# Positions instead of weights stand still in four feed-forward stages, and their product is turned on TensorE

## What is computed

```python
def swiglu(h, w13, w2):
    gate, up = jnp.split(h @ w13, 2, axis=-1)      # w13: 1024 x 5632, w2: 2816 x 1024
    return (jax.nn.silu(gate) * up) @ w2

def second_block(x, mem, positions, ...):
    for l in range(2):
        h = rms_norm_2(x, ffn1_norms[l, 0])
        x = x + 0.5 * rms_norm_2(swiglu(h, ffn1_w13[l], ffn1_w2[l]), ffn1_norms[l, 1])
        ...                                        # token mixing, cross attention
        h = rms_norm_2(x, ffn2_norms[l, 0])
        x = x + 0.5 * rms_norm_2(swiglu(h, ffn2_w13[l], ffn2_w2[l]), ffn2_norms[l, 1])
```

## Time and profile before

| | |
|---|---|
| median of 3 runs | 2096.44 us (2095.05 to 2098.67) |
| the profiled execution | 2096.13 us |
| its span, first to last instruction | 2093.9 us |
| TensorE matmul, weight load busy | 97%, 90% |
| VectorE, ScalarE, GpSimd busy | 65%, 52%, 2% |
| share of TensorE in the chain that ended last | 79% |
| weights and inputs moved | 359.30 MB, mean 172 GB/s |

### The profile page before, as it was taken

The page is one execution under the profiler, slowest core; times in us unless marked ns, Lnnn a source line. Parts: engine busy times, 40 slices in busy tenths (PEclk is TensorE's granted clock), DMA queues, the critical chain, the costliest instruction groups (busy, mean ns, idle before and its releaser), DMA issues.

```text
span 2093.9 us, 37767 instructions
## 1 busy us (share of the span) xinstructions
PE 2029.4 (97%) x15428; PEld 1894.5 (90%) x15428; DVE 1363.5 (65%) x1871; ACT 1093.0 (52%) x1702; POOL 52.3 (2%) x50
## 2 busy tenths in 40 slices
PE   7999999999999999999999999999999899998998
PEld 7989988999899889889888998999899898888997
DVE  6786866776566566767767554655477677756554
ACT  5846555554554454456456444644455455545443
POOL 0021000000000000010100000000000011000000
PEclk9999999999999999999999999999999999999999
DMA  7522454555465556434554655555555435444553
GB/s 263 171 74 82 163 186 145 203 188 187 161 221 189 186 179 203 166 111 141 181 201 145 206 184 191 199 183 183 191 183 180 157 111 169 168 166 153 182 189 121
DMA packets 98441, 359.30 MB, mean 172 GB/s; under 512 B 11160, under 2 KB 11480, under 8 KB 98008
## 3 DMA queue, kind: packets, MB, share of 16 engines
q1 hardware_dynamic: 98272, 356.90, 49.9%
HBM read 353.65 MB, written 1.05 MB: 169 GB/s over the span
## 4 chain that ended last, share of the span: by engine, by line
PE 79%; DVE 12%; ACT 6%; issue 2%; DMA 1%; ACTq 0%; SPq 0%; DVEq 0%
PE ps L923 15%; PE ps L924 14%; PE ps L925 14%; PE ps L988 6%; PE ps L989 6%; PE ps L990 6%; PE ps L911 5%; DVE wlo L1514 4%; PE ps L1067 2%; PE ps L1068 2%; PE ps L1074 2%; ACT whi L2223 2%; PE ps L955 1%; PE ps L956 1%; PE ps L957 1%
## 5 line engine op out<-in xcount | busy, mean ns | idle before, releaser
L1514 DVE TENSOR_TENSOR wlo<-raw,whi 128x1024 fp32r<-128x1024 f32 x635 | 771.2, 1224 | 497.8 <-ACT whi L2223 496.4
L2223 ACT ACTIVATE whi<-raw 128x1024 fp32r<-128x1024 f32 x635 | 665.1, 1056 | 385.8 <-PE ps L925 169.0
L923 PE MATMUL ps<-H,whi 128*128 128x256 f32 x2608 | 746.0, 286 | 1.7 <-DVE wlo L1514 1.7
L924 PE MATMUL ps<-L,whi 128*128 128x256 f32 x2608 | 737.7, 283 | 0.0
L925 PE MATMUL ps<-H,wlo 128*128 128x256 f32 x2608 | 737.7, 283 | 0.0
L923 PEld LDWEIGHTS ps<-H,whi 128*128 128x128 f32 x2608 | 500.0, 192 | 7.7 <-issue 4.7
L924 PEld LDWEIGHTS ps<-L,whi 128*128 128x128 f32 x2608 | 500.2, 192 | 0.5
L925 PEld LDWEIGHTS ps<-H,wlo 128*128 128x128 f32 x2608 | 500.1, 192 | 0.0
L988 PE MATMUL ps<-whi,HH 128*128 128x512 f32 x440 | 171.2, 389 | 0.0
L989 PE MATMUL ps<-whi,HL 128*128 128x512 f32 x440 | 171.2, 389 | 0.0
L990 PE MATMUL ps<-wlo,HH 128*128 128x512 f32 x440 | 171.2, 389 | 0.0
(11 more groups left out here) (422 smaller groups left out, 2966.3 us busy)
## 6 DMA issues: line engine op xcount, KB each, us to landing
raw<-in_ws SPq DMA_DIRECT2D x635, 512.0 KB, 3.8
prow<-in_rows SPq DMA_DIRECT2D x11, 512.0 KB, 6.0
row<-in_rows SPq DMA_DIRECT2D x9, 512.0 KB, 5.3
mema<-in_memT SPq DMA_DIRECT2D x4, 512.0 KB, 5.0
mema<-in_mem2T SPq DMA_DIRECT2D x4, 512.0 KB, 7.1
memb<-in_mem2T SPq DMA_DIRECT2D x4, 512.0 KB, 5.8
DT<-in_dec SPq DMA_DIRECT2D x2, 768.0 KB, 4.9
X<-in_x SPq DMA_DIRECT2D x1, 1024.0 KB, 9.7
```

The lines of the kernel that those rows point to most:

```text
L923: e.matmul(o, h, hs[k], start=first and k == 0, stop=False, skip_group_check=True)
L924: e.matmul(o, h, ls[k], start=False, stop=False, skip_group_check=True)
L1514: e.tensor_tensor(m.wlo[:, n % SPL, :], r, h.bitcast(F32), SUB).then_inc(*c.lo.done(n))
L2223: e.activation(m.whi[:, n % SPL, :], m.raw[:, n % RAW, :], ACT.Copy).then_inc(*c.hi.done(n))
```

## The change

In the four stages `head` and `fin` are replaced. `wide(s, g, u)` computes group g (256 gate and 256 up columns) in four units u; a unit holds the 512 columns of two rows k of `w13`. For each k and each half tb of the positions, `wide_row` makes three matmuls in which 128 positions of `H` or `L` stand still and 512 columns of `whi` or `wlo` move. The result has positions on the partitions: gate in the left half of a bank, up in the right. `wide_out` applies Silu and multiplies, 128 x 256 for each half. As `w2` needs channels on the partitions, `hidden_turned(s, g)` turns the product on TensorE (four 128 x 128 transposes), and ScalarE and VectorE write `HH` and `HL` from the turned bank. It stands behind the second unit of the next group; for the last group behind the second `out_row`.

The junction changes with it. The first four units are gone through twice: `begin(s, u)` computes group 0 for half 0 of the positions as soon as that half is split, inside the junction, and `go_on(s, u)` for half 1 afterwards; the four units stay in their slots meanwhile. `begin` 0 to 2 stand ahead of the transposes of half 1, `begin` 3 behind them. The `weights` steps are set anew. `fin_out` keeps only the form of stage `"f"` (its hunks are left out below, as are the tables that map steps to functions).

```diff
--- before.py
+++ after.py
@@ -240,7 +240,7 @@
 
         def weights(n):
 
-            o.put("weights", n + 1 - sum(step[0] in ("keys", "values") for step in o.steps[begun:]))
+            o.put("weights", n + 1 - sum(step[0] in ("keys", "values", "begin") for step in o.steps[begun:]))
 
         o.put("sqrt")
         if s == "f":
@@ -271,14 +271,26 @@
             o.put("jh", s, 0, 0)
             o.put("jh", s, 0, 1)
             o.put("jn", s, 1)
-            if fill > 2:
-                weights(4)
-            if fill:
+            if s[0] in ("a", "b"):
+                if fill:
+                    later += o.few(fill - 1)
+                for u in range(3):
+                    if fill + u > 2:
+                        weights(fill + u + 1)
+                    o.put("begin", s, u)
+                o.put("jt", s, 1)
+                o.put("jh", s, 1, 0)
+                weights(fill + 4)
+                o.put("begin", s, 3)
+                o.put("jh", s, 1, 1)
+            else:
+                if fill > 2:
+                    weights(4)
                 later += o.few(fill - 1)
-            o.put("jt", s, 1)
-            o.put("jh", s, 1, 0)
-            weights(max(fill + 2, 4))
-            o.put("jh", s, 1, 1)
+                o.put("jt", s, 1)
+                o.put("jh", s, 1, 0)
+                weights(fill + 2)
+                o.put("jh", s, 1, 1)
         o.still = False
         for step in later:
             o.put(*step)
@@ -333,6 +345,9 @@
     def ffn(p, s, behind, mid=()):
         junction(p, s, 3 if s[0] == "a" else 2 if s != ("b", 1) else 0)
         mid = list(mid)
+        if s != "f":
+            wide(s, behind, mid)
+            return
         head("fin", s)
         o.put("row", s)
         if behind:
@@ -350,6 +365,29 @@
             o.put(*step)
         for k in range(18):
             o.work("out_row", s, k)
+
+    def wide(s, behind, mid):
+        for u in range(4):
+            o.put("go_on", s, u)
+            o.put("weights", u + 2)
+        o.put("row", s)
+        if behind:
+            o.put("prow", behind)
+        for g in range(11):
+            if g:
+                for u in range(4):
+                    o.work("wide", s, g, u)
+                    if u == 1:
+                        o.put("hidden_turned", s, g - 1)
+                        if mid:
+                            o.put(*mid.pop(0))
+            o.put("wide_out", s, g)
+        for step in mid:
+            o.put(*step)
+        for k in range(18):
+            o.work("out_row", s, k)
+            if k == 1:
+                o.put("hidden_turned", s, 10)
 
     o.put("first")
     for step in mem_pieces(0):
@@ -1079,6 +1117,63 @@
             for j in range(2):
                 banks.release(*stage, j)
 
+    wide_at = {}
+
+    def wide_tiles(s, g, u):
+
+        name, layer = ffn_in(s)
+        out = []
+        for k in (2 * u, 2 * u + 1):
+            at = [tile(*full(name, layer, k, 256 * g + 128 * j + 2816 * up)) for up in range(2) for j in range(2)]
+            out.append((k, at[0]))
+        return out
+
+    def wide_row(s, g, tb, k, i, *unit):
+        h, lo = m.weight(i, 4)
+        o = banks.of("wide", s, g, tb)[:, :]
+        xh, xl = hs[k][:, 128 * tb:128 * tb + 128], ls[k][:, 128 * tb:128 * tb + 128]
+        e.matmul(o, xh, h, start=k == 0, stop=False, skip_group_check=True)
+        e.matmul(o, xh, lo, start=False, stop=False, skip_group_check=True)
+        mm = e.matmul(o, xl, h, start=False, stop=k == 7, skip_group_check=True)
+        names = [("wide", s, g, tb)] * (k == 7) + list(unit)
+        if names:
+            mm.then_inc(*pe.done(*names))
+        if k == 7:
+            banks.release("wide", s, g, tb)
+
+    def begin(s, u):
+
+        if u == 0:
+            for tb in range(2):
+                bank_for("wide", s, 0, tb, hold=True)
+        wide_at[s, u] = wide_tiles(s, 0, u)
+        if u % 2 == 0:
+            e.wait_ge(*dve.after("L", s, 0, u // 2))
+        for k, i in wide_at[s, u]:
+            wide_row(s, 0, 0, k, i)
+
+    def go_on(s, u):
+        if u % 2 == 0:
+            e.wait_ge(*dve.after("L", s, 1, u // 2))
+        for k, i in wide_at[s, u]:
+            wide_row(s, 0, 1, k, i, *[("unit", i // UT)] * (k % 2))
+
+    def wide(s, g, u):
+        if u == 0:
+            for tb in range(2):
+                bank_for("wide", s, g, tb, hold=True)
+        for k, i in wide_tiles(s, g, u):
+            for tb in range(2):
+                wide_row(s, g, tb, k, i, *[("unit", i // UT)] * (k % 2 and tb))
+
+    def hidden_turned(s, g):
+        bank = bank_for("ht", s, g)
+        e.wait_ge(*dve.after("up", s, g))
+        for j in range(2):
+            for tb in range(2):
+                t = e.transpose(pair(bank)[:, j, 128 * tb:128 * tb + 128], m.UP[g % 2][:, tb, 128 * j:128 * j + 128], C["ident"])
+        t.then_inc(*pe.done(("ht", s, g)))
+
     def keys(i, n):
         mem, mh, ml = m.mem(i)
         name, layer = mem_of(i)[2]
@@ -1951,23 +2046,36 @@
...
+    def wide_out(s, g):
+
+        if g >= 2:
+            e.wait_ge(*pe.after("ht", s, g - 2))
+        for tb in range(2):
+            e.wait_ge(*act.after("cv", s, g, tb))
+            tt(m.UP[g % 2][:, tb, :], banks.of("wide", s, g, tb)[:, 256:512], m.CV[g % 2][:, tb, :], MUL, ("up", s, g))
+            banks.free(dve, "wide", s, g, tb)
+
+    def hidden_turned(s, g):
+        e.wait_ge(*act.after("hh", s, g))
+        tt(m.HL[:, 2 * g:2 * g + 2, :], pair(banks.of("ht", s, g)), m.HH[:, 2 * g:2 * g + 2, :].bitcast(F32), SUB, ("hl", s, g))
+        banks.free(dve, "ht", s, g)
@@ -2538,22 +2646,27 @@
...
+    def wide_out(s, g):
+        if g >= 2:
+            e.wait_ge(*dve.after("up", s, g - 2))
+        for tb in range(2):
+            e.wait_ge(*pe.after("wide", s, g, tb))
+            do(m.CV[g % 2][:, tb, :], banks.of("wide", s, g, tb)[:, 0:256], ACT.Silu, ("cv", s, g, tb))
+
+    def hidden_turned(s, g):
+        e.wait_ge(*pe.after("ht", s, g))
+        do(m.HH[:, 2 * g:2 * g + 2, :], pair(banks.of("ht", s, g)), ACT.Copy, ("hh", s, g))
...
```

47 lines of the change are left out of this document (20 added, 27 removed).

## The result

| | before | after |
|---|---|---|
| median of 5 runs of each, us | 2096.44 (2095.05 to 2098.67) | 2107.83 (2104.97 to 2114.08) |
| ratio, 95% interval | | 1.0055 (1.0044 to 1.0067) |
| profiled execution, its span | 2096.13, 2093.9 | 2107.83, 2105.6 |

Both kernels were timed again three times beside the experiments: ratios of 1.0043 (1.0025 to 1.0061), 1.0034 (1.0020 to 1.0048) and 1.0035 (1.0023 to 1.0047). The mean of the four is 1.0042, 8.8 us. The prediction was 2095.6 us, no change, with a range that ended at 2102. It was wrong.

The account below looks back on a forecast made before the run. TensorE alone was taken to set the pace in the changed stages. Matmuls and transposes 5.4 us faster, junctions 4.9 us slower, so 0.5 us faster: 2095.6 us against 2096.13, with a range of 2091.5 to 2102.

Parts of the forecast that it names:

- parts 1 and 2: Changed stages: 512-column matmuls save 6.4 us a stage, added transposes cost 5.06; together 5.4 us faster for four.
- junctions of `("a", 0)`, `("b", 0)`, `("a", 1)`, full clock: Junctions ahead of the first three changed stages: four units done 2.3, 1.8 and 1.5 us later than before.
- junction of `("b", 1)`: Last junction, without filler: 1.9 us earlier at full clock, some 1.2 lost to a clock fall, net 0.7 us earlier.
- group of transposes: Four added 128x128 transposes in each of 11 groups of a stage: 0.46 us a group, bounds 0.36 and 0.60.
- Part 3: Junctions: fourth unit's conversion stands behind `H`, so TensorE idles 2.5 us before `begin` 3 at all four; together 4.9 us slower.
- rival C: New stalls at all four junctions: the granted clock falls there, 6 us in all, 2101.6 us; chance 0.14.
- the rule on transposes: Every junction: transposes don't count as matmuls for the clock, so 3.48 us between `begin` 2 and `begin` 3 are idle.
- D: Transposes of the changed stages cost their upper bound, 6.2 us more, 2101.8 us; chance 0.06.

Follow-up runs that it names:

- warm2: Changed kernel with ten extra 512-column matmuls in the stall of each junction, ahead of the wait for the fourth unit; 2103.21 us, ratio 1.0014.

## Why the prediction was wrong

Forecast for the four stages: 5.4 faster, 4.9 slower, sum -0.5. Measured, mean of four traces: 797.1 against 789.8, +7.3 us. By the steps of the prediction:

| step | forecast | measured |
|---|---|---|
| parts 1 and 2, steady, four stages | -5.4 | -4.0 |
| junctions of `("a", 0)`, `("b", 0)`, `("a", 1)`, full clock | +2.3, +1.8, +1.5 | +2.7, +2.1, +1.6 |
| the same three, clock behind the new stall | 0 | +3.2 |
| junction of `("b", 1)`, its clock included | -0.7 | +1.7 |

**Parts 1 and 2: right in kind, short by 1.4 us.** Away from the transposes the matmuls came out at the 0.2268 us of the earlier trace rows. By the gap that the Trainium skill (TensorE: Matmul & The Clock Gate, Back-to-back issue gap) gives for a single matmul the whole would have been near 2118; the rows of both kernels disagree, with 0.120 us for 256 columns and 0.227 for 512. The term that was mis-sized is the group of transposes, 0.488 us instead of 0.46: 40 x 0.028 = 1.1 us, most of it in the matmuls behind the group (the last group of a stage took 0.46). The other 0.3 us is rounding: 0.16 us a unit was 6.4 us a stage, where 115.20 less 480 x 0.2268 is 6.3. The transposes did not wait for `UP`, and no conversion was late for their sake.

**Part 3, the order of ScalarE's program: right.** The 2.5 us at all four junctions were there, 2.55. J came 5.2, 4.6 and 4.1 us later than before at the first three, forecast 4.95, 4.4 and 4.1. From J to the fifth unit it took 10.47 to 10.50 us at full clock, forecast 10.35. (The +2.1 for `("b", 0)` is from warm2, since in all four traces of the changed kernel the clock fell there.)

**The step that failed** is "2.14 us did not, and these stalls are 2.5 us", by which rival C got 0.14. I compared the new stall's length with two waits, 2.75 us with a fall and 2.14 without, and counted a length between the two as one that keeps the clock. Nothing in the rows said so, and the 2.14 us wait rested on one execution: the same wait lost the clock in 14 of 34 cases over all traces, two of eight in the kernel before. The stall also isn't 2.55 us but 3.58 from J to `begin` 3, with only eight short transposes in it, and the prediction had that number (3.48) under the rule on transposes and left it at a rival. The clock fell behind 12 of 16, three an execution at 1.6 us: 4.8 us, one of them at `("b", 1)`, where I had counted a fall behind the first wait and none behind the second. Rival C's mechanism with its price of 1.5 us was right, and right in three places of four. Whether the transposes count for the clock as matmuls do (the Trainium skill, TensorE: Matmul & The Clock Gate, Part 4, PE-mode transpose, says that they don't) no run here tells apart: warm2 put matmuls beside them, not in their place.

**The junction of `("b", 1)`**: J was 11.8 to 12.5 us behind the first transposes in the four traces, forecast 11.5 with the cold clock; with 1.6 for the second fall, 2.4 us of error in one junction.

**The range** ended at 2102 because C and D, each taken alone, gave 2101.6 and 2101.8. They don't exclude each other: C came with 1.4 us of the steady part and 0.8 us of the junctions, and with the unchanged code's own variation, which I had not put into the range at all: 1304 to 1306 us before, but up to 1312 in one trace.

## What to carry to other kernels

A step placed behind another in an engine's program waits for all that this one waits for: before a block of work is moved into a junction, list what each engine's program has between its conversions there, and move the conversions too. Here that one step was worth 18 us and the sign of the result. A stall of TensorE costs its length and, where work is thin around it, the clock behind it (1.6 us for 2.55 here, in 16 of 22 cases). One trace in which a wait kept the clock doesn't show that such a wait keeps it: look at the same wait in several traces, and until then count the fall as likely. Whether the printed wait counts or the whole time from full work to full work (2.55 or 3.58 us here) was not settled.

## What the runs showed of the hardware

- Ten useless matmuls in a 2.55 us wait kept the granted clock at 1.00 behind it at all four junctions; without them it fell behind 12 of 16 in the changed kernel.
- A 2.14 us wait in code that no edit touched had the clock fall around its end in 14 of 34 cases, a 2.75 us wait in 29 of 34.
- Code that no edit touched took 1304 to 1312 us from one trace to the next, with 7 to 27 us of it at a clock of 0.50. Two traces of one kernel differed by 6.6 us there. The part ahead of the first changed stage took 563.0 to 563.5 us in the four traces without a stretch at 0.50 in it and 564.5 to 566.0 in the other 13.
- A 128x128 transpose in a run started 0.109 us behind the one before. Four more in a group cost 0.102 each, and a group of four between matmuls of 512 columns 0.488, of which 0.04 lies in the matmuls behind it.
